# Prompt attention: where the groups of transposes stand among the scores of a half

## What is computed

```python
p_c = masked_softmax(jnp.einsum('bqkgd,bnkd->bqkgn', q, kc) * scale, m_c)
o_c = jnp.einsum('bqkgn,bnkd->bqkgd', p_c.astype(vc.dtype), vc)
p_s = masked_softmax(jnp.einsum('bqkgd,bkqmd->bqkgm', q, ks) * scale, m_s)
o_s = jnp.einsum('bqkgm,bkqmd->bqkgd', p_s.astype(vs.dtype), vs)
p_w = masked_softmax(jnp.einsum('bqkgd,bwkd->bqkgw', q, kw) * scale, m_w)
o_w = jnp.einsum('bqkgw,bwkd->bqkgd', p_w.astype(vw.dtype), vw)
return gates[..., 0:1] * o_c + gates[..., 1:2] * o_s + gates[..., 2:3] * o_w
```

## Time and profile before

| | us |
|---|---|
| median of three runs (1854.03 to 1855.23) | 1854.6 |
| span of the profiled execution | 1851.3 |
| TensorE busy / weight loads busy | 1811.8 / 1617.9 |
| VectorE busy | 1178.0 |
| ScalarE busy | 938.0 |
| GpSimd busy | 471.1 |

### The profile page before, as it was taken

One profiled execution on the slowest core, in us unless ns is written; L12 is line 12 of the kernel. 1 busy time (PEld: TensorE's weight loads), 2 busy tenths in 40 slices (PEclk: granted clock), 3 DMA queues, 4 the chain that ended last, 5 costly groups with the idle time before them and its releaser, 6 DMA issues.

```text
span 1851.3 us, 32100 instructions
## 1 busy us (share of the span) xinstructions
PE 1811.8 (98%) x11821; PEld 1617.9 (87%) x11822; DVE 1178.0 (64%) x1673; ACT 938.0 (51%) x1574; POOL 471.1 (25%) x627
## 2 busy tenths in 40 slices
PE   8999999999999999999999999999999999999998
PEld 8999999789999878888988898998867888888884
DVE  5744444556221379999999999644477686744756
ACT  4333344113021278888898888411133676645756
POOL 0000000000000025555555554002212454322431
PEclk9999999999999999999999999999999999999999
DMA  5234334214241640000000000535246797877875
GB/s 183 86 104 116 102 98 162 80 46 128 86 147 38 218 112 1 1 2 1 2 2 2 1 1 8 168 89 172 93 195 247 286 392 296 289 272 234 317 241 195
DMA packets 119762, 241.08 MB, mean 130 GB/s; under 512 B 27986, under 2 KB 84858, under 8 KB 113466
## 3 DMA queue, kind: packets, MB, share of 16 engines
q1 hardware_dynamic: 112666, 214.26, 33.0%
q0 software_dynamic: 6976, 25.17, 5.5%
HBM read 193.52 MB, written 45.88 MB: 129 GB/s over the span
## 4 chain that ended last, share of the span: by engine, by line
PE 53%; DVE 5%; ACT 3%; issue 1%; POOL 1%; DMA 0%; POOLq 0%; ACTq 0%; DVEq 0%
PE ps L3450 20%; PE ps L2169 6%; PE ps L2195 5%; PE ps L3032 4%; PE ps L263 4%; PE ps L2141 3%; PE ps L2143 3%; PE ps L3438 1%; DVE small L2286 1%; PE ps L2133 1%; PE ps L3499 1%; ACT turned_high L2397 1%; PE ps L2212 1%; ACT region_w L2386 1%; DVE turned_low L2310 1%
## 5 line engine op out<-in xcount | busy, mean ns | idle before, releaser
L2286 DVE TENSOR_REDUCE small<-ps 128x1 f32<-128x640 f32 (+7 forms) x256 | 179.5, 703 | 25.4 <-PE ps L2133 23.6
L2310 DVE TENSOR_TENSOR turned_low<-ps,turned_high 128x512 fp32r<-128x512 f32 (+2 forms) x304 | 176.6, 614 | 11.5 <-ACT turned_high L2397 7.3
L2465 POOL TENSOR_SCALAR region_w<-region_w,small,gates 128x640 f32<-128x640 f32 (+7 forms) x172 | 141.0, 831 | 127.8 <-DVE small L2290 127.7
L2397 ACT CAST turned_high<-ps 128x512 fp32r<-128x512 f32 (+2 forms) x304 | 156.3, 530 | 30.5 <-PE ps L2169 26.4
L2195 PE MATMUL ps<-turned_high,value_stacks 128*128 128x256 f32 (+1 forms) x608 | 160.4, 294 | 0.1
L2141 PE MATMUL ps<-key_stacks,query_stacks 128*128 128x256 f32 (+3 forms) x384 | 140.6, 366 | 13.3 <-ACT region_w L2386 6.7
L2195 PE MATMUL ps<-turned_low,value_stacks 128*128 128x256 f32 (+1 forms) x608 | 149.2, 282 | 0.0
L2386 ACT ACTIVATE region_w<-ps,small 128x640 f32<-128x640 f32 (+7 forms) x172 | 121.6, 707 | 23.8 <-DVE small L2286 19.9
L3450 PE MATMUL ps<-down_parts,hidden_parts 128*128 128x512 f32 x552 | 131.1, 393 | 0.0
L3450 PE MATMUL ps<-up_parts,rows_parts 128*128 128x512 f32 x552 | 129.1, 389 | 0.1
L3450 PE MATMUL ps<-gate_parts,rows_parts 128*128 128x512 f32 x528 | 126.0, 394 | 0.0
(11 more groups left out here) (558 smaller groups left out, 4900.5 us busy)
## 6 DMA issues: line engine op xcount, KB each, us to landing
region_k<-in_w_gate SPq DMA_DIRECT2D x16, 2048.0 KB, 9.3
region_k<-in_w_up SPq DMA_DIRECT2D x16, 2048.0 KB, 10.9
region_w<-in_w_down SPq DMA_DIRECT2D x16, 2048.0 KB, 13.9
region_w<-in_w_in SPq DMA_DIRECT2D x14, 512.0 KB, 4.3
region_k<-in_w_in SPq DMA_DIRECT2D x10, 512.0 KB, 4.3
small<-gate_a SPq DMA_DIRECT2D x8, 516.0 KB, 3.5
region_w<-gate_b SPq DMA_DIRECT2D x8, 516.0 KB, 4.1
region_k<-in_x_prompt SPq DMA_DIRECT2D x8, 512.0 KB, 7.7
```

Of the source, the lines that this page charges most:

```text
L2286: nc.vector.tensor_reduce(nmax[:, n % 4:n % 4 + 1], sc, AX.X, ALU.max, negate=True).then_inc(s_max, 1)
L2310: nc.vector.tensor_tensor(lo, m.ps[:, turn_bank(G), 0:w], hi, ALU.subtract).then_inc(s_lo, 1)
L2397: nc.scalar.copy(hi, m.ps[:, turn_bank(G), 0:w]).then_inc(s_hi, 1)
L2465: nc.gpsimd.tensor_scalar(probs(H, t), probs(H, t), rec[:, H % 4, t:t + 1], m.gates[:, 2 * p + t, col:col + 1], ALU.mult, ALU.mult).then_i ...
```

## The change

Two loops are written in another order. On TensorE the first group of transposes of half H stood between the two tiles' scores of half H + 2; now both tiles' scores stand first and all groups behind them. On ScalarE the first group's rounded copy stood ahead of the first exponential of half H + 2; now it stands behind it, beside the second group's. VectorE's and GpSimd's orders are as they were. No instruction is added or removed, and each waits for what it waited for.

```diff
@@ TensorE
             if H + 2 < NHALF and compressed_ahead(H + 2):
                 compressed_scores(compressed_of(H + 2), 0)
-            for G in todo[0:1]:
-                turn(G)
             if H + 2 < NHALF:
                 scores(H + 2, 1)
...
-            for G in todo[1:2]:
+            for G in todo[0:2]:
                 turn(G)
@@ ScalarE
-            for G in todo[0:1]:
-                high(G)
             if H + 2 < NHALF:
                 job_probs(H + 2, 0)
-            for G in todo[1:2]:
+            for G in todo[0:2]:
                 high(G)
```

## The result

The changed kernel takes 1894.3 us (four runs, 1891.1 to 1895.6) against 1854.9 us of the kernel before on the same chip: slower by 39 us, ratio 1.021, 95% interval 1.020 to 1.023. The profiled span grew from 1851.3 to 1889.3 us. The first scores of the last half begin 38.4 us later than before, so all of it was lost inside the attention stage. The runs' times lie 1.7 to 1.8 us above their spans wherever both are on record; of the 3.3 us named for the kernel before, the rest would then be that its profiled execution was faster than the median.

A forecast was written before the change was run, and what follows sets the result against it. TensorE, VectorE and ScalarE are all near their limit, so the path through them counts. A loss of 6.0 us a round, 0.375 a half over 126 halves, gives 47 us: 1902 us, own range 1888 to 1915, full range 1870 to 1930.

The forecast's parts named there:

- S1 waits: In a wide half TensorE's second-tile scores wait 0.62 us for the second tile's exponential; first transposes run behind.
- h0 on the path from M0 to P1: ScalarE's first rounded copy now lies between first tile's maximum and second tile's exponential, 0.48 us for 512 columns.
- VectorE waits for h0: VectorE's first low part waits for ScalarE's first rounded copy, 0.45 us late in half 51, delaying half 54's maximum.
- End of P1 to S1: From the end of the second tile's exponential to the second-tile scores it frees on TensorE: 0.20 to 0.24 us.
- the sum over the round: Attention stage, halves 57 to 72: 1.95 us for six wide halves plus 4.05 for ten, 6.0 a round.
- the walk's hand-over times: Times between engines in the round's step-by-step sum, good to some 0.05 us, three in each half's path.
- The narrow term: Halves 51 to 53: TensorE's second group of transposes, values and next scores come 1.34 us late, 0.45 a half.
- the signs: A middle round takes about 66 us; exponentials wait about 1 us a half for maxima; copies no longer wait for TensorE.
- Only some halves lose: Lag absorbed where the first maximum does not hold the first exponential: 2.6 us a round, 21 in all, 1875; chance 0.14.
- Faster: ScalarE's waits ahead of copies and the scores' waits for exponentials go: 13 us less, 1842; chance 0.05.
- No change: TensorE is the bound and its instructions are the same: 1854; chance 0.05.
- The clock: New waits in halves 51 to 56 lower TensorE's clock once a round, 3.4 us lost, 27 in all, 1929; chance 0.10.

The follow-up runs named there:

- e2: Kernel before with only ScalarE's move, the first rounded copy behind the first exponential, TensorE's order as before: 1878.7 us, ratio 1.013.
- w1: Kernel before with the change only in loop turns with H mod 16 from 8 to 15: 1873.0 us, ratio 1.010.
- n1: Kernel before with the change only in loop turns with H mod 16 from 0 to 7: 1880.8 us, ratio 1.015.
- e3: Changed kernel with ScalarE's second exponential moved ahead of the third group's rounded copy: 1916.6 us, ratio 1.033.
- e5: Changed kernel with VectorE's low parts of the third and fourth group moved behind the next half's first maximum: 1897.6 us, ratio 1.024.

## Why the prediction was right

The time, 1894.3 us, lies in the range (1870 to 1930) and in the forecast's own (1888 to 1915). The mechanism held in these steps, which the traces can show:

- *S1 waits.* It does in the wide half as well, and T0 comes behind the wait. e2 against the changed kernel prices TensorE's move at 1.6 us a round.
- *h0 on the path from M0 to P1.* ScalarE waits for M0 with nothing to fill the time. From P0 of half 60 to P1 it is 2.31 us; I had 2.41 (three copies 1.31 instead of 1.41 us). In half 52, P0 to P1 is 1.93 us, forecast 1.94.
- *VectorE waits for h0.* 0.34 us ahead of l0 in half 51, for which I had l0 0.45 us late, and 0.61 us in half 52. From l0 of half 51 to the maximum of half 54 it is 1.77 us in both kernels (876.25 to 878.02, 892.94 to 894.71), so the maximum is late by all that l0 is.
- *End of P1 to S1.* 0.23 us in both places; I took 0.20 and 0.23.

**What was mis-sized** is the sum over the round: 6.0 us forecast, 4.75 measured; 47 us in all against 38 in the span. In the order of the forecast, the first scores of halves 60 to 65 came later by +0.25, +0.06, +0.58, +0.05, +0.30, +0.12 us each, together 1.36, where I had 1.95; the ten behind them 3.38, where I had 4.05. The largest of the six came out (0.58 for 0.61), one was larger (0.30 for 0.19), and four were smaller, above all 0.12 for 0.40 and 0.25 for 0.42; the time is right in part because the range was wide enough for that. The runs of copies were one such term (0.10 us too much for three of them, above); for the rest the walk's hand-over times are the likely place, which no run separates. The narrow term worked out from the old state, 1.34 us over the halves 51 to 53, is 1.70 (0.35, 0.42 and 0.93): the sum was not too high there. Of the signs, three were too strong: a round is 64.9 us and not 66, the exponentials wait 10.5 us a round for maxima, 0.66 a half and not 1, and ScalarE's copies still wait 1.5 us a round for transposes.

**The rivals.** *Only some halves lose*: w1 has 2.1 us a round from the wide halves alone, where this rival had two waits of 0.62, 1.24 us. *Faster*: ScalarE's waiting for transposes did shrink, from 2.9 to 1.5 us a round, and it bought nothing, since the exponentials' waiting, nearly all for maxima, rose from 4.7 to 11.8 us. *No change*, and with it the reading by the highest busy share: VectorE's share in the round fell from 92 to 85%, with the same work in the same order. The Trainium skill's page "Perfetto Trace Analysis" says in its section "Optimization Strategy" that one then looks for the gaps of the engine taken as the bound and for what ends them; by that the trace agrees, since VectorE's largest gaps in the changed kernel's round, 6.2 us ahead of low parts, are ended by ScalarE's copies. *The clock*: in the changed kernel one more fall, in the first round, which is 5.3 us longer than before against 4.75 for the others, so about half a microsecond of the profiled executions' 38. That execution was the fastest of the four, though: the other three took 2 to 4.5 us more at a mean granted clock of 0.991 to 0.993 in place of 0.995, so the clock may have some 3 us of the changed kernel's median; where in those runs it fell is not on record. In n1, w1 and e3 this rival's mechanism became true, at 1.4 us a fall in n1, where I had 3.4.

## What to carry to other kernels

With several engines near full that hand each other work in every turn of a loop, follow the longest path from one turn's start to the turn after next, and see what each engine does while it waits: an instruction moved out of such a wait costs time even if nothing is added, here less than its length (e2: 0.20 us a half for copies of 0.36 to 0.48). A moved pair of instructions on two engines should be judged together: each of these two moves alone costs 66 and 25 us, together 39. And compare rounds in which the clock is the same before adding up effects; the medians of n1 and w1 alone speak for a carried lag, and the rounds without a fall add up to the whole.

## What the hardware showed that was not expected

The granted clock of TensorE fell to 1.2 GHz inside a stage in which it is busy over 90% of the time, with no long idle time ahead. In n1 the longest wait in the 6 us before a fall was 1.4 us each time, in w1 0.7 us. From the second round on, a fall cost 1.35 to 1.54 us of time where a round has one (n1: 64.15 against 62.76; w1: 63.64 and 63.80 against 62.26; e5: 66.60 against 65.25), while the second fall in a round of e3 added 0.56 (68.43 against 67.87).

The waits that are seen do not tell which round has a fall. In n1 the clock fell behind a stretch with 2.74 of 4 us busy; in the round before it stayed up behind 2.79 of 4 at the like place, and also behind the stretch that begins 1.8 us later:

```profile
827.00:831.00 4.00, 2.40 (x17) 1.69 (x17) 3.31 (x9) 3.27 (x9) 1.49 (x3) 1.00 0.01 2
```

The changed kernel has the same wait of 1.4 us in every round and more waits in all than n1 (a round of 64.9 against 62.8 us), and it had no fall from the second round to the seventh, where n1 had four.
